# Expert layer: next block turned one weight unit ahead, first expert's rows selected by matmuls on chip

## The chip, the cores and the metric

One core of one Trainium2 chip. The time is device microseconds (us) of one execution. PE is TensorE (PEld its weight load), ACT is ScalarE, DVE is VectorE, POOL is GpSimd, SP is SyncE, which issues most DMAs.

## The reference, cut to what matters

Two decoder layers run on 256 prompt rows and 8 sample rows, 264 rows of 1024 numbers. Layer 1 ends in a layer of 8 experts: each row goes to the two experts with the highest router logits.

```python
logits = h @ w_router + b_router
top_v, top_i = lax.top_k(logits, 2)
gates = softmax(top_v)
for e in range(8):
    act = silu(h @ we_gate[e]) * (h @ we_up[e])
    out = out + combine[..., e:e + 1] * (act @ we_down[e])
```

`h` is RMSNorm(x) of the layer's rows; an expert's hidden width is 1408. All numbers are float32.

## The kernel before, in words

**Numbers in two parts.** Every large product is made of three: an operand is split into a high part (rounded to float32r, a form of float32 that PE takes in one pass) and a low part (what the rounding left), and high x high, high x low and low x high are added in PSUM. For weights, ACT writes the high part (`whi`, lines 899 and 1085) and DVE the low part (`low`, line 309) of a *unit*, up to 2048 columns on 128 partitions, 1 MB. `raw` and `low` share six buffers, `whi` has three: high part c waits until unit c-3 has been used by PE (line 1084), and the DMA of unit c (line 430) until unit c-6 has (line 423).

**The experts.** An expert is 18 units (lines 94 to 102): gate and up projections (units 0 to 7, and 10 to 13), down projections (8, 9, and 14 to 17). Expert 0 is written out, experts 1 to 7 run in a loop on each engine. Work on one expert needs its block of 128 chosen rows, transposed: `ehi` and `elo`, 8 tiles of 128x128 in high and low parts. The next expert's block is made near the end of the one before: PE transposes it out of `xe` in `gather_turn` (lines 782 to 786, before the flow of units 16 and 17), ACT writes `ehi` out of PSUM (`take_turned`, 1087 to 1091, its last step of an expert) and DVE `elo` (`turned_low`, 1655 to 1660, likewise). Only then do ACT and DVE split the next expert's units. PE's first product of an expert waits for `ehi`, `elo` and unit 0 (lines 825 to 829).

**The routing ahead of expert 0.** When the last group of layer 1 is done, PE transposes x into token rows (`route_turns`, 502 to 508; half 0 into PSUM banks 1 to 3, half 1 into 4 to 6) and makes the router's logits; DVE takes the rows' statistics (1212 to 1219), picks two experts per row, and works out in `offf` and `offi` where each row goes (lines 1594 to 1632). ACT writes the normed token rows `xn` (1114). POOL scatters them to the DRAM buffer `xs` with six indirect DMAs (1877 to 1881); SP waits for all six, then reads block 0 back into `xe` (417, 418). PE transposes it (866) and expert 0 begins.

Of the kernel before, what the change touches and what calls it, by code (L numbers as in the profile page):

```python
# [22 lines left out]
P = 128  # L23
D = 1024
KT = D // P
# [3 lines left out]
DEPTH = 2  # L29
# [88 lines left out]
LG0, BI0, RK0 = 0, 32, 64  # L118
COLS0 = 272
# [5 lines left out]
def build(nc, a, out):  # L125
    ctx = ExitStack()
    with ctx:
# [7 lines left out]
        with ExitStack() as same:  # L135
# [84 lines left out]
        xn = sb("xn", [P, 3, D], where=moe)  # L220
        picked = sb("picked", [P, 2, 3, D], where=moe)
# [25 lines left out]
        cnti = sb("cnti", [P, 1], I32, where=moe)  # L247
        moe.close()
# [32 lines left out]
            "row_out", "col_ps", "col_done", "zero_done", "filled", "xn_done", "xtok_done", "off_done", "scattered", "gates_done", "fin_gain",  # L281
# [72 lines left out]
        def _(sp):  # L354
# [96 lines left out]
        def _(pe):  # L451
# [282 lines left out]
            for l in range(DEPTH):  # L734
# [47 lines left out]
            def gather_turn(it):  # L782
                pe.wait_ge(S["xe_in"], it * 16 + 16)
# [4 lines left out]
            def expert(it):  # L788
# [36 lines left out]
                pe.wait_ge(S["ehi_done"], it + 1)  # L825
                pe.wait_ge(S["elo_done"], it + 1)
# [28 lines left out]
                turn_hidden(2, 2)  # L855
                down(15)
                gather_turn(it + 1)
# [5 lines left out]

            pe.wait_ge(S["xtok_done"], 6)
            pe.wait_ge(S["off_done"], 1)
            gather_turn(0)
# [12 lines left out]
        def _(act):  # L879
# [207 lines left out]
            def take_turned(it):  # L1087
                act.wait_ge(S["xeT_ps"], it + 1)
                for k in range(KT):
                    last = act.activation(ehi[:, k, :], ps[:, 6 + k // 4, (k % 4) * P:(k % 4 + 1) * P], ACT.Copy, scale=N_(k, NORM_ROW[3]))  # L1090
                last.then_inc(S["ehi_done"], 1)
# [19 lines left out]
            for j, (_, n) in enumerate(TILES):  # L1111
                for half in range(2):
                    c = slice(half * PB, (half + 1) * PB)
                    act.activation(xn[0:n, j, c], token_rows(j, half, n), ACT.Copy, scale=rcol[0:n, j:j + 1]).then_inc(S["xn_done"], 1)
            expert_hi(0, 2)
            act.wait_ge(S["top_done"], 1)
            act.activation(gt[:, :, 1:2], gt[:, :, 0:1], ACT.Exp).then_inc(S["gate_exp"], 1)
# [45 lines left out]
            take_turned(0)  # L1163
            expert(0)
# [19 lines left out]
        def _(dve):  # L1184
# [111 lines left out]
            def layer(l):  # L1296
# [233 lines left out]
                else:  # L1530
                    expert_lo(0, 0)
                    expert_lo(0, 1)
                dve.wait_ge(used, U + 12)
# [41 lines left out]
            dve.wait_ge(S["moe_const"], 4)  # L1575
            dve.wait_ge(S["stored"], 16 * STORES * DEPTH)
            dve.wait_ge(S["cs_out"], 64 * DEPTH)
            dve.wait_ge(S["tT_ps"], 1)
            token_statistics(0)
# [52 lines left out]
            dve.tensor_copy(offi[:, :], offf[:, :]).then_inc(S["off_done"], 1)  # L1632

# [12 lines left out]
            dve.tensor_copy(cnti[:, :], cnt[:, 2:3]).then_inc(S["rounds"], 1)  # L1646
            expert_lo(0, 2)
# [7 lines left out]
            def turned_low(it):  # L1655
                dve.wait_ge(S["ehi_done"], it + 1)
                for k in range(KT):
                    last = dve.scalar_tensor_tensor(elo[:, k, :], ps[:, 6 + k // 4, (k % 4) * P:(k % 4 + 1) * P], N_(k, NORM_ROW[3]),  # L1658
                                                    ehi[:, k, :].bitcast(F32), ALU.mult, ALU.subtract)
                last.then_inc(S["elo_done"], 1)  # L1660
# [40 lines left out]
            turned_low(0)  # L1701
# [29 lines left out]
        def _(pool):  # L1731
# [140 lines left out]
            settle()  # L1872
            pool.memset(chosen[:, :, :], 0.0).then_inc(S["moe_const"], 1)
# [41 lines left out]
```

## Time and profile before

| | |
|---|---|
| median of 3 runs | 1043.75 us (1042.79 to 1044.28) |
| the profiled execution | 1043.59 us, of which the span of instructions is 1041.8 us |
| busy | PE 890.4 us (85%), DVE 756.9 (73%), ACT 540.2 (52%), POOL 181.4 (17%) |
| chain that ended last | PE 68%, DVE 23%, DMA 3%, issue 3%, ACT 3% |
| DMA | 240.38 MB, mean 231 GB/s; 322 to 368 GB/s in the slices from 600 us to the end of the experts |

A row of the trace gives when an instruction started, how long it took, and in brackets how long its engine had been idle and what ended that. Rows of PE overlap: the distance between two starts is what a product costs in a stream. The granted clock is 1.00 at 2.4 GHz and 0.50 at 1.2 GHz.

### The profile page before, as it was taken

The page shows a single profiled execution, that of the slowest core. Times are in us where ns is not written, and L with a number is a line of the kernel's source. Part 1 is how long each engine was busy: PE and PEld are TensorE (multiplying, and loading weights), DVE is VectorE, ACT ScalarE, POOL GpSimd, SP SyncE. Part 2 cuts the span into 40 slices and gives each one's busy share as a digit, 9 for nine tenths or more (in the row PEclk, how much of TensorE's full clock was granted, in tenths as well). Part 3 has the DMA queues.
Part 4 walks back from the last instruction along what each step waited for, and adds up shares of the span by engine and source line. Part 5 has one row for each costly group of instructions (what it writes and reads, how often), then busy time and mean ns, then how long its engine had stood idle before and what let it go on. Part 6 is the DMA issues. An engine that isn't in the chain of part 4 may idle for free.

```text
span 1041.8 us, 14010 instructions
## 1 busy us (share of the span) xinstructions
PE 890.4 (85%) x5260; PEld 775.1 (74%) x5260; DVE 756.9 (73%) x945; ACT 540.2 (52%) x541; POOL 181.4 (17%) x228
## 2 busy tenths in 40 slices
PE   4967777899999999877786498989898989898970
PEld 3965746899999999867475387878787878787860
DVE  3599986465566346899866287878788888788856
ACT  5425631444344335265323277667677777677750
POOL 1299123300000002992231100000000000000001
PEclk9989878899999999998688699999999999999995
DMA  9470104996536559611044399999999999999933
GB/s 308 136 234 21 62 10 125 365 414 213 182 118 226 169 179 265 214 40 42 11 135 148 129 353 335 356 322 366 326 361 341 362 345 368 333 354 348 357 131 125
DMA packets 116749, 240.38 MB, mean 231 GB/s; under 512 B 12772, under 2 KB 35062, under 8 KB 116685
## 3 DMA queue, kind: packets, MB, share of 16 engines
q1 hardware_dynamic: 107213, 207.28, 57.8%
q0 software_dynamic: 8048, 27.16, 7.5%
q10 hardware_dynamic: 1440, 5.28, 1.3%
q8 instruction: 33, 0.54, 0.2%
q14 instruction: 15, 0.12, 0.0%
HBM read 214.23 MB, written 26.04 MB: 231 GB/s over the span
## 4 chain that ended last, share of the span: by engine, by line
PE 68%; DVE 23%; DMA 3%; issue 3%; ACT 3%; POOL 0%; POOLq 0%; ACTq 0%; DVEq 0%
PE ps L537 9%; PE ps L538 9%; PE ps L539 9%; PE ps L799 8%; PE ps L801 8%; PE ps L800 8%; DVE low L309 3%; PE ps L813 3%; PE ps L815 3%; PE ps L814 3%; DVE ac L1233 3%; DVE cb L1233 2%; DVE Cs L1474 2%; ACT ehi L1090 1%; DVE elo L1658 1%
## 5 line engine op out<-in xcount | busy, mean ns | idle before, releaser
L309 DVE TENSOR_TENSOR low<-raw,whi 128x2048 fp32r<-128x2048 f32 (+2 forms) x204 | 433.5, 2135 | 109.5 <-ACT whi L1085 63.0
L1085 ACT ACTIVATE whi<-raw 128x2048 fp32r<-128x2048 f32 (+1 forms) x144 | 254.2, 1781 | 96.2 <-PE ps L801 57.0
L537 PE MATMUL ps<-nhi,whi 128*128 128x264 f32 x736 | 216.3, 294 | 11.2 <-DVE low L309 6.3
L538 PE MATMUL ps<-nlo,whi 128*128 128x264 f32 x736 | 213.7, 290 | 0.0
L539 PE MATMUL ps<-nhi,low 128*128 128x264 f32 x736 | 212.6, 289 | 0.0
L899 ACT ACTIVATE whi<-raw 128x2048 fp32r<-128x2048 f32 (+1 forms) x60 | 109.4, 1825 | 119.0 <-PE ps L539 119.0
L799 PE MATMUL ps<-whi,ehi 128*128 128x512 f32 (+1 forms) x384 | 149.1, 388 | 22.5 <-DVE low L309 18.0
L537 PEld LDWEIGHTS ps<-nhi,whi 128*128 128x128 f32 x736 | 143.6, 195 | 14.0 <-issue 12.4
L801 PE MATMUL ps<-whi,elo 128*128 128x512 f32 (+1 forms) x384 | 146.8, 382 | 0.0
L800 PE MATMUL ps<-low,ehi 128*128 128x512 f32 (+1 forms) x384 | 146.7, 382 | 0.0
L538 PEld LDWEIGHTS ps<-nlo,whi 128*128 128x128 f32 x736 | 143.7, 195 | 0.1
L539 PEld LDWEIGHTS ps<-nhi,low 128*128 128x128 f32 x736 | 142.9, 194 | 0.0
L799 PEld LDWEIGHTS ps<-whi,ehi 128*128 128x128 f32 x384 | 73.8, 192 | 37.4 <-ACT whi L1085 20.8
L801 PEld LDWEIGHTS ps<-whi,elo 128*128 128x128 f32 x384 | 73.8, 192 | 12.0
L800 PEld LDWEIGHTS ps<-low,ehi 128*128 128x128 f32 x384 | 74.0, 193 | 11.6
L1885 POOL TENSOR_TENSOR cnt<-cnt 128x1 f32<-128x1 f32 x1 | 0.2, 193 | 435.7 <-DMA xs<-ysb 435.7
L813 PE MATMUL ps<-whi,fhi 128*128 128x512 f32 x176 | 71.6, 407 | 5.1 <-DVE flo L1679 5.1
L815 PE MATMUL ps<-whi,flo 128*128 128x512 f32 x176 | 69.5, 395 | 0.0
L814 PE MATMUL ps<-low,fhi 128*128 128x512 f32 x176 | 69.4, 394 | 0.0
L1797 POOL TENSOR_SCALAR Cp<-apad,prm 128x256 f32<-128x256 f32 x48 | 52.9, 1111 | 0.0
L538 PE MATMUL ps<-hlo,whi 128*128 128x264 f32 x176 | 50.1, 284 | 0.0
L537 PE MATMUL ps<-hhi,whi 128*128 128x264 f32 x176 | 50.0, 284 | 0.0
(367 smaller groups left out, 1226.7 us busy)
## 6 DMA issues: line engine op xcount, KB each, us to landing
raw<-in_we_down SPq DMA_DIRECT2D x40, 1024.0 KB, 6.1
raw<-in_we_gate SPq DMA_DIRECT2D x32, 1024.0 KB, 7.5
raw<-in_we_up SPq DMA_DIRECT2D x32, 1024.0 KB, 7.0
raw<-in_w_in SPq DMA_DIRECT2D x16, 1024.0 KB, 5.9
xs<-zero POOLq DMA_DIRECT2D x5, 2560.0 KB, 30.2
raw<-in_we_gate SPq DMA_DIRECT2D x16, 768.0 KB, 7.5
raw<-in_we_up SPq DMA_DIRECT2D x16, 768.0 KB, 5.7
raw<-in_w_gate SPq DMA_DIRECT2D x10, 1024.0 KB, 5.2
```

The source lines that it names most:

```text
L309: return engine.tensor_tensor(low[:, u % NRAW, part], raw[:, u % NRAW, part], whi[:, u % NHI, part].bitcast(F32), ALU.subtract)
L537: pe.matmul(o, hi[:, k, c], xhi[:, kx, :], start=first, stop=False)
L538: pe.matmul(o, hi[:, k, c], xlo[:, kx, :], start=False, stop=False)
L539: last = pe.matmul(o, lo[:, k, c], xhi[:, kx, :], start=False, stop=end)
L799: pe.matmul(bank(b, w), ehi[:, k0 + k, :], hi[:, k, :], start=(k0 + k == 0), stop=False)
L800: pe.matmul(bank(b, w), ehi[:, k0 + k, :], lo[:, k, :], start=False, stop=False)
L801: last = pe.matmul(bank(b, w), elo[:, k0 + k, :], hi[:, k, :], start=False, stop=(k0 + k == KT - 1))
L813: pe.matmul(bank(4 + half), fh, hi[:, k, s], start=(t == 0), stop=False)
L814: pe.matmul(bank(4 + half), fh, lo[:, k, s], start=False, stop=False)
L815: last = pe.matmul(bank(4 + half), fl, hi[:, k, s], start=False, stop=(t == 10))
L899: act.activation(whi[:, u % NHI, 0:n], raw[:, u % NRAW, 0:n], ACT.Copy).then_inc(hi_done, 1)
L1085: act.activation(whi[:, c % NHI, 0:kt * w], raw[:, c % NRAW, 0:kt * w], ACT.Copy).then_inc(hi_done, 1)
```

## The change

**Next block one unit ahead.** In every expert PE runs `gather_turn(it + 1)` right after `turn_hidden(2, 2)`, before unit 15 instead of after it. `take_turned` and `turned_low` now signal after each half (4 of 8 tiles), so that DVE can start on the first half while ACT does the second.

**Expert 0's rows on chip.** ACT first writes the normed token rows as a float32r high part `thi`, DVE the low part `tlo`; DVE compares `offf` with a row of places 0 to 127 and gets `sel`, a matrix of zeros and ones (128 rows of a tile by 128 places). For each of 8 column tiles and 3 row tiles PE multiplies `thi` and `tlo` with `sel` and adds them up: 48 products of 128 columns, which leave the transposed block in banks 7 and 0. `xn` follows, each piece after its `tlo`; the scatter stays, for the experts that follow. SP no longer reads block 0; its wait for the scatter moves to where it reads block 1 (ahead of unit 10 of expert 0).

**Order around it.** PE's `route_turns(0)` moves ahead of the last weight unit of layer 1, DVE's statistics of that half too; high part 2 of expert 0, its low part and the exponential of the gates move behind `take_turned(0)` and `turned_low(0)`. `thi` and `tlo` lie where `picked` is at the end of the program.

```diff
@@ stream, on SP
                     if c == NRAW and isinstance(it, int) and it == 0:
-                        sp.wait_ge(S["scattered"], 96)
-                        sp.dma_start(xe[:, :], xs[0]).then_inc(S["xe_in"], 16)
+                        sp.wait_ge(S["moe_const"], 5)
                         sp.dma_start(gain[:, :], ...)
                     if c == 10:
+                        if isinstance(it, int) and it == 0:
+                            sp.wait_ge(S["scattered"], 96)
                         sp.wait_ge(S["xeT_ps"], it + 1)
                         sp.dma_start(xe[:, :], block_of(xs, it + 1)).then_inc(S["xe_in"], 16)
@@ end of layer 1, on PE
                     group(25, nhi, nlo, (0,))
                     route_logits(0)
+                    route_turns(0)
                     group(25, nhi, nlo, (1,))
-                    route_turns(0)
@@ expert, on PE
-                pe.wait_ge(S["ehi_done"], it + 1)
-                pe.wait_ge(S["elo_done"], it + 1)
+                pe.wait_ge(S["elo_done"], it * 2 + 2)
...
                 down(14)
                 turn_hidden(2, 2)
+                gather_turn(it + 1)
                 down(15)
-                gather_turn(it + 1)
@@ ahead of expert 0, on PE
+            pe.wait_ge(S["sel_done"], 3)
+            for j, (_, n) in enumerate(TILES):
+                for half in range(2):
+                    pe.wait_ge(S["tT_lo"], 2 * j + half + 1)
+                    for k in range(4 * half, 4 * half + 4):
+                        o, d = ps[:, FIRST_TURNED[half], (k % 4) * P:(k % 4 + 1) * P], slice(k * P, (k + 1) * P)
+                        pe.matmul(o, thi[0:n, j, d], sel[0:n, j, :], start=(j == 0 and k % 4 == 0), stop=False)
+                        last = pe.matmul(o, tlo[0:n, j, d], sel[0:n, j, :], start=False, stop=(j == 2 and k % 4 == 3))
+            last.then_inc(S["xeT_ps"], 1)
             pe.wait_ge(S["xtok_done"], 6)
-            pe.wait_ge(S["off_done"], 1)
-            gather_turn(0)
@@ take_turned, on ACT (turned_low on DVE alike)
-                for k in range(KT):
-                    last = act.activation(ehi[:, k, :], ps[:, 6 + k // 4, ...], ACT.Copy, scale=N_(k, NORM_ROW[3]))
-                last.then_inc(S["ehi_done"], 1)
+                for half in range(2):
+                    b = FIRST_TURNED[half] if isinstance(it, int) and it == 0 else 6 + half
+                    for k in range(4 * half, 4 * half + 4):
+                        last = act.activation(ehi[:, k, :], ps[:, b, ...], ACT.Copy, scale=N_(k, NORM_ROW[3]))
+                    last.then_inc(S["ehi_done"], 1)
@@ after the places are known, on DVE
+            for j, (_, n) in enumerate(TILES):
+                step(dve.tensor_scalar(sel[0:n, j, :], places[0:n, :], offf[0:n, 2 * j:2 * j + 1], None, ALU.is_equal))
+            settle()
+            for j, (_, n) in enumerate(TILES):
+                dve.scalar_tensor_tensor(sel[0:n, j, :], places[0:n, :], offf[0:n, 2 * j + 1:2 * j + 2], sel[0:n, j, :].bitcast(F32),
+                                         ALU.is_equal, ALU.add).then_inc(S["sel_done"], 1)
+            for j, (_, n) in enumerate(TILES):
+                for half in range(2):
+                    c = slice(half * PB, (half + 1) * PB)
+                    dve.wait_ge(S["tT_hi"], 2 * j + half + 1)
+                    dve.scalar_tensor_tensor(tlo[0:n, j, c], token_rows(j, half, n), rcol[0:n, j:j + 1], thi[0:n, j, c].bitcast(F32),
+                                             ALU.mult, ALU.subtract).then_inc(S["tT_lo"], 1)
```

How the rows of three places stand, by engine. First PE in the loop over the experts, from the transposes of the last hidden tiles (`hm`) to unit 16; before:

```order
L821 MATMUL ps<-ident,hm 128x128 [waits hm_done]
L821 MATMUL ps<-ident,hm 128x128 x2
...
L813 MATMUL ps<-whi,fhi 128x512 [waits lo_done,hi_done]
L814 MATMUL ps<-low,fhi 128x512
L815 MATMUL ps<-whi,flo 128x512
...
L785 MATMUL ps<-ident,xe 128x128 [waits xe_in]
L785 MATMUL ps<-ident,xe 128x128 x7
```

and in the change:

```order
L828 MATMUL ps<-ident,hm 128x128 [waits hm_done]
L828 MATMUL ps<-ident,hm 128x128 x2
...
L792 MATMUL ps<-ident,xe 128x128 [waits xe_in]
L792 MATMUL ps<-ident,xe 128x128 x7
...
L820 MATMUL ps<-whi,fhi 128x512 [waits lo_done,hi_done]
L821 MATMUL ps<-low,fhi 128x512
L822 MATMUL ps<-whi,flo 128x512
```

The eight transposes of the next block (`xe`) have moved in front of the twelve products of unit 15.

DVE between the places of the rows (`offi`) and expert 0; before:

```order
L1632 CAST offi<-offf 128x6 [waits dve_step]
L1638 COPY xtok<-ps 128x512 [waits xn_done] x4
L1638 COPY xtok<-ps 8x512 [waits xn_done] x2
...
L309 TENSOR_TENSOR low<-raw,whi 128x2048 [waits hi_done]
...
L1658 SCALAR_TENSOR_TENSOR elo<-ps,prm,ehi 128x128 [waits ehi_done]
L1658 SCALAR_TENSOR_TENSOR elo<-ps,prm,ehi 128x128 x7
```

and in the change:

```order
L1662 CAST offi<-offf 128x6 [waits dve_step]
L1664 TENSOR_SCALAR sel<-places,offf 128x128 x2
L1664 TENSOR_SCALAR sel<-places,offf 8x128
L1667 SCALAR_TENSOR_TENSOR sel<-places,offf,sel 128x128 [waits dve_step]
L1667 SCALAR_TENSOR_TENSOR sel<-places,offf,sel 128x128
L1667 SCALAR_TENSOR_TENSOR sel<-places,offf,sel 8x128
L1673 SCALAR_TENSOR_TENSOR tlo<-ps,rcol,thi 128x512 [waits tT_hi] x4
L1673 SCALAR_TENSOR_TENSOR tlo<-ps,rcol,thi 8x512 [waits tT_hi] x2
L1680 COPY xtok<-ps 128x512 [waits xn_done] x4
L1680 COPY xtok<-ps 8x512 [waits xn_done] x2
...
L1606 SCALAR_TENSOR_TENSOR elo<-ps,prm,ehi 128x128 [waits ehi_done]
```

Twelve instructions, `sel` and `tlo`, stand new ahead of the copies `xtok`, and `elo` comes ahead of low part 2.

ACT from the square root of the statistics to expert 0; before:

```order
L1109 ACTIVATE rcol<-ms 128x3 [waits ms_done]
L1114 ACTIVATE xn<-ps,rcol 128x512 [waits col_done]
L1114 ACTIVATE xn<-ps,rcol 128x512 x3
L1114 ACTIVATE xn<-ps,rcol 8x512 x2
L1085 ACTIVATE whi<-raw 128x2048 [waits unit_used,raw_in2]
L1117 ACT_TABLE_LOAD
L1117 ACTIVATE gt<-gt 128x3 [waits top_done]
L1090 ACTIVATE ehi<-ps,prm 128x128 [waits xeT_ps]
```

and in the change:

```order
L1124 ACTIVATE rcol<-ms 128x3 [waits ms_done]
L1129 ACTIVATE thi<-ps,rcol 128x512 [waits col_done]
L1129 ACTIVATE thi<-ps,rcol 128x512 x3
L1129 ACTIVATE thi<-ps,rcol 8x512 x2
L1134 ACTIVATE xn<-ps,rcol 128x512 [waits tT_lo] x4
L1134 ACTIVATE xn<-ps,rcol 8x512 [waits tT_lo] x2
L1105 ACTIVATE ehi<-ps,prm 128x128 [waits xeT_ps]
L1098 ACTIVATE whi<-raw 128x2048 [waits unit_used,raw_in2]
```

The six `thi` stand where `xn` stood, `xn` waits for the low parts, and high part 2 comes behind `ehi`.

## Rows read from the trace of the kernel before

**Rows 1.** Windows; columns: window, length, busy (count) PE PEld DVE ACT POOL, clock, DMA, GB/s
```profile
567.00:583.00 16.00, 0.05 (x3) 0.00 (x0) 8.01 (x23) 4.40 (x6) 7.58 (x6) 0.50 0.49 186
...
589.50:593.50 4.00, 4.00 (x10) 3.13 (x11) 0.00 (x0) 0.00 (x0) 0.00 (x0) 0.50 0.00 0
```

**Rows 2.** Chain of waits from 558 to 625 us; columns: start, length, what
```profile
577.26 2.49 DMA xs<-xn,offi
...
579.76 3.15 DMA xe<-xs
...
583.05 1.95 PE ps L785 x8
...
589.50 0.77 PE ps L799
```

**Rows 3.** Timeline of DVE and ACT during the routing; columns: start, length, instruction [idle <-releaser]
```profile
558.25 1.25 DVE L1534 TENSOR_TENSOR xT<-xT,ps 128x1056 f32<-128x1056 f32 x1 [3.64 <-PE ps L539]
...
559.66 3.67 DVE L1215 BATCH_NORM_STATS2 bst<-ps 128x6 f32<-128x512 f32 x6 [0.15 <-PE ps L507]
...
568.54 0.17 DVE L1632 CAST offi<-offf 128x6 uint32<-128x6 f32 x1
...
568.62 3.66 DVE L1638 COPY xtok<-ps 128x512 f32<-128x512 f32 x6
...
564.58 3.53 ACT L1114 ACTIVATE xn<-ps,rcol 128x512 f32<-128x512 f32 x6 [0.24 <-DVE rcol L1592]
```

**Rows 4.** Timeline of PE: two 264-column products in a row; two 128-column products
```profile
546.85 0.28 PE L537 MATMUL ps<-nhi,whi 128*128 128x264 f32 x1
...
546.97 0.28 PE L538 MATMUL ps<-nlo,whi 128*128 128x264 f32 x1
...
480.67 0.38 PE L624 MATMUL ps<-qT,kT 128*128 128x128 f32 x2
...
480.89 0.60 PE L623 MATMUL ps<-qT,kT 128*128 128x256 f32 x2
```

**Rows 5.** Waits of PE from 560 us on; columns: total us, times, longest
```profile
PE ps L799 <- DVE low L309: 18.0, 7, 2.6
```

**Rows 6.** Timeline of PE, ACT and DVE where expert 0 ends and expert 1 begins
```profile
635.23 1.04 PE L785 MATMUL ps<-ident,xe 128*128 128x128 f32 x8
...
643.01 0.47 PE L799 MATMUL ps<-whi,ehi 128*128 128x512 f32 x1 [2.57 <-DVE low L309]
...
633.03 1.05 ACT L1085 ACTIVATE whi<-raw 128x1024 fp32r<-128x1024 f32 x1
...
636.30 2.18 ACT L1090 ACTIVATE ehi<-ps,prm 128x128 fp32r<-128x128 f32 x8 [2.22 <-PE ps L785]
...
638.32 5.56 ACT L1085 ACTIVATE whi<-raw 128x2048 fp32r<-128x2048 f32 x3
...
634.39 1.22 DVE L309 TENSOR_TENSOR low<-raw,whi 128x1024 fp32r<-128x1024 f32 x1
...
638.51 2.16 DVE L1658 SCALAR_TENSOR_TENSOR elo<-ps,prm,ehi 128x128 fp32r<-128x128 f32 x8 [2.90 <-ACT ehi L1090]
...
640.59 6.69 DVE L309 TENSOR_TENSOR low<-raw,whi 128x2048 fp32r<-128x2048 f32 x3
```

**Rows 7.** Windows: three whole experts, and 3.4 us after a stop
```profile
749.20:802.50 53.30, 50.22 (x229) 41.74 (x229) 42.82 (x33) 37.08 (x34) 0.00 (x0) 0.97 0.95 341
...
802.50:854.50 52.00, 48.81 (x230) 40.69 (x230) 42.88 (x33) 37.26 (x34) 0.00 (x0) 1.00 1.00 354
...
854.50:906.30 51.80, 48.68 (x229) 40.66 (x230) 42.86 (x33) 37.13 (x34) 0.00 (x0) 1.00 1.00 353
...
695.90:699.30 3.40, 3.40 (x9) 2.66 (x10) 3.40 (x2) 0.80 (x1) 0.00 (x0) 0.51 0.96 343
```

**Rows 8.** Window: four microseconds with weights queued
```profile
656.00:660.00 4.00, 4.00 (x20) 3.18 (x19) 3.41 (x4) 2.32 (x2) 0.00 (x0) 1.00 1.00 401
```

**Rows 9.** Waits of ACT from 590 to 1005 us
```profile
ACT whi L1085 <- DMA raw<-in_we_down: 6.8, 6, 1.8
```

More of the change, by code:

```diff
@@ L118 @@
 LG0, BI0, RK0 = 0, 32, 64
+FIRST_TURNED = (7, 0)
 COLS0 = 272
@@ L220, in build @@
         xn = sb("xn", [P, 3, D], where=moe)
+        with ExitStack() as early:
+            thi = sb("thi", [P, 3, D], F32R, where=early)
+            tlo = sb("tlo", [P, 3, D], F32R, where=early)
         picked = sb("picked", [P, 2, 3, D], where=moe)
@@ L247, in build @@
         cnti = sb("cnti", [P, 1], I32, where=moe)
+        places = sb("places", [P, P], where=moe)
+        sel = sb("sel", [P, 3, P], F32R, where=moe)
         moe.close()
@@ L1088, in take_turned @@
                 act.wait_ge(S["xeT_ps"], it + 1)
-                for k in range(KT):
-                    last = act.activation(ehi[:, k, :], ps[:, 6 + k // 4, (k % 4) * P:(k % 4 + 1) * P], ACT.Copy, scale=N_(k, NORM_ROW[3]))
-                last.then_inc(S["ehi_done"], 1)
+                for half in range(2):
+                    b = FIRST_TURNED[half] if isinstance(it, int) and it == 0 else 6 + half
+                    for k in range(4 * half, 4 * half + 4):
+                        last = act.activation(ehi[:, k, :], ps[:, b, (k % 4) * P:(k % 4 + 1) * P], ACT.Copy, scale=N_(k, NORM_ROW[3]))
+                    last.then_inc(S["ehi_done"], 1)
             def y_rows(it):
@@ L1113, in _ @@
                     c = slice(half * PB, (half + 1) * PB)
+                    act.activation(thi[0:n, j, c], token_rows(j, half, n), ACT.Copy, scale=rcol[0:n, j:j + 1]).then_inc(S["tT_hi"], 1)
+            for j, (_, n) in enumerate(TILES):
+                for half in range(2):
+                    c = slice(half * PB, (half + 1) * PB)
+                    act.wait_ge(S["tT_lo"], 2 * j + half + 1)
                     act.activation(xn[0:n, j, c], token_rows(j, half, n), ACT.Copy, scale=rcol[0:n, j:j + 1]).then_inc(S["xn_done"], 1)
-            expert_hi(0, 2)
-            act.wait_ge(S["top_done"], 1)
-            act.activation(gt[:, :, 1:2], gt[:, :, 0:1], ACT.Exp).then_inc(S["gate_exp"], 1)
             def expert(it):
@@ L1163, in _ @@
             take_turned(0)
+            expert_hi(0, 2)
+            act.wait_ge(S["top_done"], 1)
+            act.activation(gt[:, :, 1:2], gt[:, :, 0:1], ACT.Exp).then_inc(S["gate_exp"], 1)
             expert(0)
@@ L1532, in layer @@
                     expert_lo(0, 1)
+                    dve.wait_ge(S["moe_const"], 5)
+                    dve.wait_ge(S["stored"], 16 * STORES * DEPTH)
+                    dve.wait_ge(S["cs_out"], 64 * DEPTH)
+                    dve.wait_ge(S["tT_ps"], 1)
+                    token_statistics(0)
                 dve.wait_ge(used, U + 12)
@@ L1574, in _, with turned_low @@
             layer(1)
[L1575 to L1579, printed above, removed]
+            def turned_low(it):
+                for half in range(2):
+                    b = FIRST_TURNED[half] if isinstance(it, int) and it == 0 else 6 + half
+                    dve.wait_ge(S["ehi_done"], it * 2 + half + 1)
+                    for k in range(4 * half, 4 * half + 4):
+                        last = dve.scalar_tensor_tensor(elo[:, k, :], ps[:, b, (k % 4) * P:(k % 4 + 1) * P], N_(k, NORM_ROW[3]),
+                                                        ehi[:, k, :].bitcast(F32), ALU.mult, ALU.subtract)
+                    last.then_inc(S["elo_done"], 1)
             dve.wait_ge(S["tT_ps"], 2)
@@ L1634, in _ @@
             for j, (_, n) in enumerate(TILES):
+                step(dve.tensor_scalar(sel[0:n, j, :], places[0:n, :], offf[0:n, 2 * j:2 * j + 1], None, ALU.is_equal))
[4 more added lines that the diff above has]
+            for j, (_, n) in enumerate(TILES):
+                for half in range(2):
+                    c = slice(half * PB, (half + 1) * PB)
+                    dve.wait_ge(S["tT_hi"], 2 * j + half + 1)
+                    dve.scalar_tensor_tensor(tlo[0:n, j, c], token_rows(j, half, n), rcol[0:n, j:j + 1], thi[0:n, j, c].bitcast(F32),
+                                             ALU.mult, ALU.subtract).then_inc(S["tT_lo"], 1)
+            for j, (_, n) in enumerate(TILES):
                 for half in range(2):
@@ L1653, in _ @@
             dve.tensor_tensor(gt[:, :, 3:4], gt[:, :, 1:2], gt[:, :, 2:3], ALU.mult).then_inc(S["gates_done"], 1)
[L1655 to L1660, printed above, removed]
             def expert(it):
@@ L1872, in _ @@
             settle()
+            pool.iota(places[:, :], pattern=[[1, P]], base=0, channel_multiplier=0, allow_small_or_imprecise_dtypes=True).then_inc(S["moe_const"], 1)
             pool.memset(chosen[:, :, :], 0.0).then_inc(S["moe_const"], 1)
```

6 lines of the change are left out of this document (3 added, 3 removed).

## The prediction

> **What bounds the kernel now.** I read the windows first, to see where PE stands still; then the chain of waits and the timelines at those places; then windows of single experts, to see what else is near its limit. Nothing before 545 us is touched by the change, nor the last 33 us, so the answer lies in two places.
>
> The first is the way from routing to expert 0. From 567 to 583 us PE is busy 0.05 us [rows 1]. The chain shows why: the last scatter lands (from 577.26 us, 2.49 us), block 0 is read back (3.15 us), PE turns it (8 transposes in 1.95 us), ACT and DVE write `ehi` and `elo`, and the first product starts at 589.50 [rows 2]. For its first 4 us the clock is granted at 0.50, which is 1.2 GHz [rows 1].
>
> The second is the border between experts. PE waits there seven times, 18.0 us in total [rows 5]; the border after expert 0 stands for all. The transposes start at 635.23, `ehi` takes ACT 2.18 us, `elo` takes DVE 2.16 us after that, and only at 640.59 does DVE come to low part 0; PE resumes at 643.01 after 2.57 us [rows 6]. Work that three engines do one after another stands in front of a unit that they could split meanwhile. Some of these stops cost twice: after the one at 693 us the clock is 0.51 for 3.4 us, in which PE starts 9 products [rows 7]. That costs half of 3.4 us, 1.7 us. Of the six experts between borders, three (one stands in the rows, 53.30 us at a mean clock of 0.97) hold such a dip, and undisturbed ones last 51.8 to 52.0 us [rows 7].
>
> **The border, step by step,** on the clock of the old trace. With the transposes ahead of unit 15 they are over at about 633.4, while ACT still makes high part 17 (633.03 for 1.05 us, to 634.1 [rows 6]). ACT then writes `ehi` at once instead of idling 2.22 us: halves at 635.2 and 636.3. DVE is free at 635.6 (low part 17, 634.39 for 1.22 us [rows 6]) and follows half by half, done at 637.8. What is late next is unit 15, pushed back by 0.9 us of transposes: its `whi` buffer is the one that high part 0 needs, so ACT starts that at 636.3 and ends at 638.2 (1.85 us each, three in 5.56 us [rows 6]); low part 0 takes 2.2 us (three in 6.69 us [rows 6]), to 640.5. PE, finished at 640.45, goes on at about 640.7. The stop shrinks from 2.57 to about 0.3 us: 2.3 us at each of seven borders, 16.1 us. Even stops of 2.57 us are followed by a dip only at three of the borders [rows 7], so at 0.3 us I take none: three dips less, 5.1 us. Together 21.2 us.
>
> That is not free of the DMA. An undisturbed expert moves 354 GB/s for 52.0 us, 18.4 MB, with the DMA engines busy all the time [rows 7]. PE alone would need 52.0 - 2.6 = 49.4 us. If 354 GB/s is the ceiling, no border gives anything in an undisturbed expert. If it is the 401 GB/s of four microseconds with weights queued [rows 8], 18.4 MB take 45.9 us and nothing is lost. I take the middle, 377 GB/s or 48.8 us: PE stays the slower one on the mean, but only just, and weights arrive unevenly. ACT already waits for down weights, six times and up to 1.8 us [rows 9], and the shorter border takes 2.3 us of slack from those units. For this I give back 0.8 us per expert, 5.6 us in seven, nearer to none than to all, because today's waits hardly reach PE. The experts then save 15.4 us; the ends are 21.2 and, at a ceiling of 354 GB/s, the dips' 5.1.
>
> The Trainium skill speaks against this part: "DMA: Bandwidth & Descriptors", section "Where 436 GB/s comes from", puts the HBM side at about 358 GB/s per core. By that figure 18.4 MB take an estimated 51.4 us per expert and the borders would give almost nothing. The trace's 401 GB/s over 4 us does not agree with such a limit, its 353 and 354 over whole experts do.
>
> **Routing.** *The moved turns.* Twelve transposes of `route_turns(0)` (0.11 us each: eight at full clock are busy for 1.04 us with the last one's tail [rows 6]) go ahead of the last weight unit, 1.3 us. Before, they ran beside the addition at 558.25 (1.25 us [rows 3]). In exchange three of six statistics (3.67 us for six [rows 3]) leave the path. From the addition's start to the last statistic took 5.08 us; now 1.25 for the addition, 1.5 for the other twelve transposes and 1.85 for three statistics, 4.7. Net the routing gets 1.0 us *later*: `offi` is ready at 569.7, not 568.7.
>
> *The selection on DVE.* Six `sel` operations of 128 columns, priced at most like `elo` (2.16 us for 8 [rows 6]), 1.6 us; six `tlo` out of PSUM like the `xtok` copies (3.66 us for 6 [rows 3]), 3.7 us. They start at 569.7 and end at 575.0. ACT's `thi` replaces `xn` one for one (3.53 us [rows 3]) and hides there. Then come the copies `xtok` (3.7 us) and the counts (0.5), so DVE cannot begin `elo` before 579.2.
>
> *The selection on PE.* No row shows a float32r product of 128 columns. Bounds at 2.4 GHz: 0.06 us, the 264-column product of 0.12 us [rows 4] scaled to 128 columns; and 0.22 us, a plain float32 product of that shape, which the trace shows as two passes of 0.11 us [rows 4]. I take one pass, 0.11 us: it is one record of the same shape, and 128 columns may not amortise a weight load that 264 do. At 1.2 GHz I take 0.244 us (the transposes of rows 2). PE starts at 571.9 after 4 us of rest, so at 1.2 GHz; as before expert 0 [rows 1] I give it 4.0 us there, 16 products, and the other 32 take 3.5 us: the block is there at 579.4. `ehi` 2.2 us, the second half of `elo` 1.1 us behind it, and PE starts expert 0 at 582.9 instead of 589.5. **Saved: 6.6 us.** With 0.06 us DVE's copies decide, and it starts at 581.5 (8.0 saved); with 0.22 us the block is there at 584.5 and it starts at 587.9 (1.6 saved).
>
> The Trainium skill ("TensorE: Matmul & The Clock Gate", section "Back-to-back issue gap") gives about 81 ns per product of 128 columns with its weight load. By that, 48 products take an estimated 3.9 us and the start lies near the early bound. No run here shows that form.
>
> *What costs nothing.* The scatter now starts when `xn` does, some 4 us later, and ends near 584; SP wants it for block 1, ahead of unit 10, which is four units of PE work, some 13 us, after 582.9. High and low part 2 fall behind `elo` and are done by 586, while PE works on units 0 and 1 until 590. The earlier load of `gain` uses DMA engines that are half idle [rows 1]. If these covers went, each would cost PE its own lateness, a few us once.
>
> **Sum.** 1043.6 us (the profiled execution; 0.2 us under the median, which I leave aside) - 15.4 - 6.6 = **1021.6 us**. With every cost at its low end 1043.6 - 21.2 - 8.0 = 1014.4; at its high end 1043.6 - 5.1 - 1.6 = 1036.9.
>
> **Rivals.** *Weights at the ceiling.* The DMA cannot exceed 354 GB/s and takes the place of the border. For it: DMA share 1.00 in both undisturbed experts [rows 7]. Against: 401 GB/s [rows 8], and no PE stop but the border in them that the weights cause. 1043.6 - 5.1 - 6.6 = 1031.9. The rule of the Trainium skill quoted above would lead to this case.
>
> *Dear selection.* The 128-column products cost 0.22 us. For it: every plain product of that shape does [rows 4]. Against: the 264-column float32r rows run twice as fast per column. 1043.6 - 15.4 - 1.6 = 1026.6.
>
> *Border unchanged.* Something other than the row turns holds unit 0, so the stop stays; 1043.6 - 6.6 = 1037.0. Against it: every step of that border is accounted for above.
>
> *Slower.* With no rest at the border the queue of weights never empties and the rate itself falls. The experts last 419.7 us now (589.5 to 1009.2). They undo the 6.6 us if they average 53.3 us, that is below 345 GB/s; at the 341 GB/s of the dipped expert [rows 7] they take 54.0 us each, 12 us more, and the total is 1049. Against it: that expert was slow because PE asked for less, and the fuller ones run at 353 and 354.
>
> **Numbers.** Forecast 0.60, ceiling 0.19, dear selection 0.14, border unchanged 0.04, slower 0.03. The range reaches from the low end, 1014, past the ceiling case to 1032, and leaves out the last two cases and part of the mixed one, in which ceiling and dear selection meet. A difference under 0.2% is about what a measurement of this kernel cannot tell from none. Faster 0.96, same 0.01, slower 0.03.
>
> **What would show it.** Right: seven border waits under 0.5 us each, none under a dipped clock; first expert product near 583; ACT waiting longer for weights than the rows of today, PE stops of about a microsecond at the first down unit. Wrong: experts of 51.5 us or more at a DMA share of 1.00 (ceiling); the 48 products spread over 12 us (dear selection); the border waits still over 2 us; or a PE start after 589.5.

## The result, and the profile after

The changed kernel takes **1020.42 us** (median of 4 runs, 1018.20 to 1021.47) against 1044.01 us of the kernel before (4 runs, 1042.79 to 1044.59): a ratio of 0.9773, with a 95% interval of 0.9752 to 0.9793. The forecast was 1021.6 us. The total fits, but it comes from two terms that were wrong by about as much in opposite directions.

| us | before | after | difference |
|---|---|---|---|
| span of the profiled execution | 1041.8 | 1016.4 | -25.4 |
| up to expert 0's first product | 589.50 | 586.43 | -3.1 |
| experts, first to last product | 419.7 | 397.6 | -22.1 |
| behind the last product | 32.65 | 32.41 | -0.2 |

The border first. The waits of PE between 585 and 990 us in the trace of the changed kernel (total us, times, longest), which answer to [rows 5]:

```profile
PE ps L820 <- DVE flo L1716: 4.4, 8, 0.6
PE ps L806 <- issue: 3.5, 1, 3.5
PE ps L806 <- DVE low L315: 1.6, 7, 0.2
```

18.0 us in seven waits have become 1.6 us; the longest is 0.2. The timeline where expert 0 ends and expert 1 begins (start, length, instruction, idle before it) answers to [rows 6]:

```profile
629.38 1.04 PE L792 MATMUL ps<-ident,xe 128*128 128x128 f32 x8
...
629.97 1.05 ACT L1098 ACTIVATE whi<-raw 128x1024 fp32r<-128x1024 f32 x1
630.87 0.55 DVE L1716 TENSOR_TENSOR flo<-ps,fhi 128x384 fp32r<-128x384 f32 x1
630.92 2.16 ACT L1105 ACTIVATE ehi<-ps,prm 128x128 fp32r<-128x128 f32 x8
631.34 1.22 DVE L315 TENSOR_TENSOR low<-raw,whi 128x1024 fp32r<-128x1024 f32 x1
632.47 2.15 DVE L1606 SCALAR_TENSOR_TENSOR elo<-ps,prm,ehi 128x128 fp32r<-128x128 f32 x8
635.21 2.29 DVE L315 TENSOR_TENSOR low<-raw,whi 128x2048 fp32r<-128x2048 f32 x1 [0.59 <-ACT whi L1098]
...
637.65 0.47 PE L806 MATMUL ps<-whi,ehi 128*128 128x512 f32 x1 [0.22 <-DVE low L315]
```

ACT goes from high part 17 (L1098 at 629.97) into `ehi` without a pause, where it had stood 2.22 us. Low part 0 still ends last, but PE stands 0.22 us for it instead of 2.57.

Windows (length, busy time of PE, PEld, DVE, ACT and POOL, clock, DMA share, GB/s) from the routing to expert 3 answer to [rows 1] and [rows 7]; the last two are whole experts (1 and 3):

```profile
567.00:583.00 16.00, 10.90 (x52) 10.56 (x52) 11.70 (x39) 6.39 (x12) 5.71 (x6) 0.59 0.34 136
586.40:590.40 4.00, 3.97 (x9) 3.14 (x10) 2.72 (x4) 2.06 (x3) 0.00 (x0) 0.50 0.02 4
...
637.65:687.17 49.52, 48.72 (x230) 40.66 (x230) 43.00 (x32) 37.39 (x34) 0.00 (x0) 1.00 1.01 373
736.65:786.18 49.53, 48.73 (x230) 40.68 (x230) 43.00 (x32) 37.28 (x34) 0.00 (x0) 1.00 0.99 365
```

An expert takes 49.5 us at a clock of 1.00 and moves its weights at 365 to 373 GB/s. None of the seven periods from one expert's first product to the next one's (49.46 to 49.67 us, and 51.2 for expert 0, which starts at the low clock) holds a further clock dip. The transfers had not been at a ceiling.

Now the routing, in the chain of waits from 556 to 600 us, which answers to [rows 2] and [rows 3]:

```profile
559.89 1.26 DVE xT L1559
561.20 1.54 PE ps L514 x12
562.76 1.89 DVE bst L1235 x3
...
570.02 0.58 DVE sel L1664 x3
570.63 0.86 DVE sel L1667 x3
571.49 0.67 DVE tlo L1673
572.30 0.45 PE ps L876
573.17 0.21 PE ps L877
...
582.96 3.47 issue
586.43 0.77 PE ps L806
```

Scatter and read-back are gone from the chain. In their place stand the 48 selection products, 572.30 to 582.96 us, and behind them 3.47 us that the view calls issue and that are `ehi` and `elo`. The products are 0.21 us apart but for one step of 0.35, where those with 8 rows begin. The window that holds them alone, between that of the 5 us before 570 and that of the 396 us from 590.4 on, says at which clock:

```profile
565.00:570.00 5.00, 0.55 (x7) 0.38 (x7) 4.05 (x33) 3.81 (x8) 0.00 (x0) 0.99 0.11 44
...
572.30:583.00 10.70, 10.66 (x48) 10.35 (x48) 7.11 (x14) 3.86 (x7) 5.71 (x6) 0.50 0.51 202
...
590.40:986.00 395.60, 387.63 (x1824) 323.56 (x1822) 336.95 (x253) 294.75 (x263) 0.00 (x0) 1.00 0.97 354
```

The granted clock was 0.50, that is 1.2 GHz, for all 48. It fell at 569.9 us (the 0.99 of the first window), when PE had been busy for 0.55 of the 5 us before, and came back at 590.4, four microseconds into expert 0.

### The profile page after: what moved, and what is told of

The parts are those of the page before. It is cut to its first block, busy times and chain, and to the rows that moved or that the text cites. A ratio compares the mean times of both kernels' runs of the same rounds, so it can differ in the third digit from the quotient of the medians.

```text
span 1016.4 us, 14109 instructions
## 1 busy us (share of the span) xinstructions
PE 895.7 (88%) x5300; PEld 780.7 (77%) x5300; DVE 764.1 (75%) x957; ACT 544.9 (54%) x547; POOL 179.8 (18%) x229
## 4 chain that ended last, share of the span: by engine, by line
PE 72%; DVE 22%; ACT 3%; issue 2%; DMA 1%; POOL 0%; POOLq 0%; DVEq 0%; ACTq 0%
PE ps L544 10%; PE ps L545 9%; PE ps L546 9%; PE ps L806 8%; PE ps L808 8%; PE ps L807 8%; DVE low L315 3%; PE ps L820 3%; PE ps L822 3%; PE ps L821 3%; DVE ac L1253 3%; DVE cb L1253 2%; PE ps L664 1%; ACT whi L1098 1%; DVE Cs L1494 1%
## 5 line engine op out<-in xcount | busy, mean ns | idle before, releaser
L1098 ACT ACTIVATE whi<-raw 128x2048 fp32r<-128x2048 f32 (+1 forms) x144 | 254.9, 1775 | 85.4 <-PE ps L808 38.0
L806 PE MATMUL ps<-whi,ehi 128*128 128x512 f32 (+1 forms) x384 | 147.0, 383 | 5.1 <-issue 3.5
```

The lines of the kernel that those rows point to most:

```text
L806: pe.matmul(bank(b, w), ehi[:, k0 + k, :], hi[:, k, :], start=(k0 + k == 0), stop=False)
L1098: act.activation(whi[:, c % NHI, 0:kt * w], raw[:, c % NRAW, 0:kt * w], ACT.Copy).then_inc(hi_done, 1)
```

## The experiments

All twelve ran beside runs of the kernel before on the same chip; ratios are to those. Where a start moves by a microsecond or two, medians of runs that spread over 2 to 3 us are a poor ruler. I also use the time within the profiled execution from the first addition to `xT` behind the last mixer (DVE; 544.48 us before, 544.84 after) to expert 0's first product: 45.02 us before, 41.59 after, and 41.58 to 41.67 in the four other kernels with the change's routing unaltered. The expectations call it the xT-to-first-product time.

### One half of the change at a time

`border_only` is the kernel before with these edits (ACT and DVE hand over `ehi` and `elo` in halves as in the change):

```diff
-                down(15)
                 gather_turn(it + 1)
+                down(15)
```

> Edit: the kernel before, with only the border half of the change (next block turned one unit ahead of down(15), ehi and elo signalled in halves); the routing and the reading back from DRAM stay. Theory (what the trace of the changed kernel shows is additive: 22.1 us of its 25.4 us lie between the first and the last expert product): about 1044.0 - 22 = 1022 us, expert periods 49.5 us, borders 0.2 us, and the first expert product still near 589.5 us. The prediction's own term (21.2 us less 5.6 us given back to the weight transfers): 1028.6 us with periods near 50.5 us. Rival (the earlier start of the experts or the removed DRAM traffic is what lets the weights keep up): periods above 50.5 us here although the border is the same.

1023.47 us (1022.33 to 1024.31), ratio 0.9789 (0.9760 to 0.9818). The experts take 398.7 us and their windows are those of the changed kernel:

```profile
690.00:740.00 50.00, 49.20 (x233) 41.16 (x232) 43.53 (x33) 37.48 (x34) 0.00 (x0) 1.00 1.01 369
```

So this half is worth 21 us by itself, on the old read-back; 1.1 us of that are the halves at expert 0, as the traces of the next run show. The give-back of 5.6 us to the transfers is not there, nor does the border need the other half.

`routing_only` is the changed kernel with the border undone (DVE's wait for `ehi` alike):

```diff
-                gather_turn(it + 1)
                 down(15)
+                gather_turn(it + 1)
...
-                    last.then_inc(S["ehi_done"], 1)
+                    if isinstance(it, int) and it == 0:
+                        last.then_inc(S["ehi_done"], 1)
+                    elif half == 1:
+                        last.then_inc(S["ehi_done"], 2)
```

> Edit: the changed kernel with the border put back (turn behind down(15), ehi and elo handed over whole; the first block keeps its halves). Theory: the routing half alone is worth what the first expert product moved, 589.50 to 586.43: 3.1 us, so about 1041 us, with the border wait of 2.6 us back at seven borders. The prediction's term was 6.6 us: 1037.4 us. Rival: the routing half alone is worth nothing, 1044 us, since the weights that it starts sooner are waited for later.

1040.38 us (1039.27 to 1042.52), ratio 0.9962 (0.9946 to 0.9978): 4 us, and 3.4 us by the xT-to-first-product time (41.58 us). The seven stops at the border are back:

```profile
PE ps L806 <- DVE low L315: 17.9, 7, 2.6
```

Not all of the 3.4 us is the selection. With the old routing that time was 45.02 us in the kernel before and 43.87 in `border_only`, and the timelines show where the two part, first the kernel before, then `border_only`:

```profile
585.03 2.18 ACT L1090 ACTIVATE ehi<-ps,prm 128x128 fp32r<-128x128 f32 x8 [13.60 <-PE ps L785]
...
587.24 2.16 DVE L1658 SCALAR_TENSOR_TENSOR elo<-ps,prm,ehi 128x128 fp32r<-128x128 f32 x8 [11.83 <-ACT ehi L1090]
```

```profile
587.38 2.17 ACT L1090 ACTIVATE ehi<-ps,prm 128x128 fp32r<-128x128 f32 x8 [13.53 <-PE ps L785]
...
588.55 2.16 DVE L1659 SCALAR_TENSOR_TENSOR elo<-ps,prm,ehi 128x128 fp32r<-128x128 f32 x8 [10.72 <-ACT ehi L1090]
```

From the places (`offi`) to PE's transposes both take the same, 14.51 and 14.44 us, so the read-back is constant. From the start of `ehi` to the first product it is 4.47 us before and 3.39 in `border_only`, where `elo` follows half by half. There, ahead of expert 0, PE waits for `elo` itself, and the halves are worth 1.1 us; the selection with its moved turns is worth the other 2.3 us (43.87 to 41.59). Both runs hold the halves at expert 0, so their gains, 20.9 and 4.0 us, count this 1.1 us twice, which is most of what they add up to above the 23.6 of the whole change.

### Which part of the border

`no_halves` keeps the early turn and hands `ehi` and `elo` over whole (the second piece of the diff above); `turn_late` keeps the halves and turns behind `down(15)` (the first piece).

> Edit: the changed kernel, where ehi and elo of the next block are again handed over whole and not in halves; the turn stays ahead of down(15). Theory (the unit of down products of about 2.6 us that now lies behind the turn hides the 2.57 us by itself): the border grows from 0.2 us to at most 1.2 us, 1020.4 to 1027 us, most likely near 1021. Rival (both parts are needed): each border about 1.1 us, which is half of ACT's eight copies of 2.2 us, 1028 us, or more where clock dips return.

1020.20 us (1019.19 to 1021.04), ratio 0.9759 (0.9730 to 0.9789), as fast as the changed kernel, with the same waits at the border:

```profile
PE ps L806 <- DVE low L315: 1.6, 7, 0.2
```

> Edit: the changed kernel with the turn put back behind down(15); ehi and elo stay in halves. Theory: the halves hide about 1.1 us of the old border wait of 2.57 us, so each of seven borders keeps 1.2 to 1.5 us: 1020.4 + 7 x 1.35 = 1030 us, and 1035 us if the three clock dips return. Rival (the halves alone would have done): within 2 us of the changed kernel, 1022 us.

1038.11 us (1035.17 to 1039.60), ratio 0.9932 (0.9910 to 0.9955). The theory expected 1030 to 1035, since the halves would hide 1.1 us of each border. They hide 0.26: PE's waits there are 16.1 us over seven borders, where `routing_only` has 17.9.

```profile
PE ps L806 <- DVE low L315: 16.1, 7, 2.3
```

The timeline of the border at 740 us says why:

```profile
738.01 2.17 ACT L1105 ACTIVATE ehi<-ps,prm 128x128 fp32r<-128x128 f32 x8 [2.21 <-PE ps L792]
...
739.18 2.16 DVE L1606 SCALAR_TENSOR_TENSOR elo<-ps,prm,ehi 128x128 fp32r<-128x128 f32 x8 [2.11 <-ACT ehi L1105]
...
740.02 5.56 ACT L1098 ACTIVATE whi<-raw 128x2048 fp32r<-128x2048 f32 x3
...
742.02 4.49 DVE L315 TENSOR_TENSOR low<-raw,whi 128x2048 fp32r<-128x2048 f32 x2 [0.68 <-ACT whi L1098]
...
744.46 0.47 PE L806 MATMUL ps<-whi,ehi 128*128 128x512 f32 x1 [2.30 <-DVE low L315]
```

`elo` is done at 741.3, but DVE then waits 0.68 us for high part 0, which ACT makes after all of `ehi`. What PE waits for is the next unit's split behind the turn, not the turn. Halves shorten a handover that does not end last; the early turn moves ACT's whole queue forward. All of the border's gain is the one moved line; halves pay only where PE waits for `elo` itself, ahead of expert 0. The total came out above the theory because 2.3 us remain at each border and two of the three clock dips are back in the trace (0.50 and 0.52 for 3.4 us from 951.9 and from 692.6 us). `turn_late` also shows that a DMA share near 1 proves no ceiling: the expert from 744.46 to 796.05 us has a share of 0.99 at 355 GB/s, those after the change 1.01 at 373.

### How near the transfers are

`no_low_weights` leaves out the products with the weights' low parts in all experts, a third of PE's work there (the low parts are still made):

```diff
-                        pe.matmul(bank(b, w), ehi[:, k0 + k, :], lo[:, k, :], start=False, stop=False)
...
-                            pe.matmul(bank(4 + half), fh, lo[:, k, s], start=False, stop=False)
```

> Edit: the changed kernel without the products of the low part of the weights in all experts (a third of PE's work there is left out; the low parts are still made). Theory (the weight transfers still have room at the changed kernel's period of 49.5 us, 371 GB/s): the period falls, to the 43 us that DVE is busy per expert or to 46 us, which is 18.4 MB at the 401 GB/s seen in one window of the kernel before; 8 x 4 = 28 us off, near 990 us. Rival (with the border gone the transfers are the bound, as the DMA share of 1.0 in the changed kernel's windows suggests): the period stays at 49 to 49.5 us, 1016 to 1020 us. Third (the ceiling of 354 GB/s that the prediction allowed): 52 us, which the changed kernel has already gone below.

1000.15 us (a single run). With PE out of the way an expert takes 47.4 to 47.9 us and not the 43 or 46 hoped for; one of them:

```profile
777.36:825.03 47.67, 38.79 (x160) 29.41 (x160) 42.65 (x33) 36.95 (x34) 0.00 (x0) 0.93 1.03 387
```

No engine is busy all the time, the DMA is, at 387 GB/s, and ACT now waits for weights, 25.9 us in four experts against 8.0 us in five of the changed kernel; half of it are the down weights:

```profile
ACT whi L1096 <- DMA raw<-in_we_down: 13.3, 13, 2.0
```

The changed kernel's 49.5 us are thus PE's, with some 2 us per expert between them and this rate. The room is there, but little of it is left. Whether the transfers could do more than 387 GB/s over an expert no run here shows.

### What the selection costs

`turns_back` puts the first twelve turns and their statistics back:

```diff
-                    route_turns(0)
                     group(25, nhi, nlo, (1,))
+                    route_turns(0)
```

> Edit: the changed kernel with the first twelve turns to token rows and their statistics put back behind the last unit, as before. Theory (the move costs the routing 0.95 us: from the first xT addition to the places 25.01 us after, 24.06 before): the first expert product comes 0.95 us sooner, 1019.5 us. Rival (the twelve turns that no longer stand ahead of PE's last unit keep PE busy later, and the statistics, three of 0.62 us, come behind it): 0 to 1 us later, 1020.4 to 1021.4 us.

1020.75 us (1020.70 to 1021.00), ratio 0.9769 (0.9743 to 0.9796). In the trace `offi` comes 24.06 instead of 25.01 us after the addition and the first product 40.65 instead of 41.59, as expected; the total doesn't show it. One part of it went back to the clock, which rose 4.8 instead of 4.0 us after the first product: expert 0's first six units, up to its first turn of hidden columns, took 19.46 instead of 19.05 us. The rest is inside the spread between runs.

`halfwise` orders low parts, products, rows and copies by halves of the columns, with a signal behind the first half:

```diff
-            for j, (_, n) in enumerate(TILES):
-                for half in range(2):
-                    pe.wait_ge(S["tT_lo"], 2 * j + half + 1)
+            for half in range(2):
+                for j, (_, n) in enumerate(TILES):
+                    pe.wait_ge(S["tT_lo"], 3 * half + j + 1)
...
-            last.then_inc(S["xeT_ps"], 1)
+                last.then_inc(S["half_ps"] if half == 0 else S["xeT_ps"], 1)
```

> Edit: the changed kernel with the low parts, the selection products, the normalised rows and the row copies in the order half by half (all three token tiles of columns 0 to 511, then of 512 to 1023) and a signal behind the first half, so that ACT and DVE take ehi and elo of it while PE selects the other. Theory: of the 3.47 us between the last selection product and the first expert product 1.1 to 1.6 us go (half of ACT's and DVE's eight copies of 2.17 us each): xT-to-first-product 40.2 instead of 41.6 us, 1019.1 us. Rival (ACT or DVE is busy with rows and copies then, so nothing moves): 1020.4 us.

1019.23 us (1018.13 to 1021.24), ratio 0.9750 (0.9723 to 0.9777); 40.95 instead of 41.59 us to the first product. The gap behind the products shrinks from 3.47 to 2.44 us, but the products end 0.4 us later behind the places, since PE now changes between 128-row and 8-row products three times instead of once, and each time the next two starts are 0.34 and 0.27 us apart instead of 0.21.

`awake` adds products that nobody reads, so that PE does not rest:

```diff
+            def keep_awake(n, b):
+                for _ in range(n):
+                    pe.matmul(bank(b, PB), nhi[:, 0, 0:P], whi[:, 0, 0:PB], start=True, stop=True)
...
             last.then_inc(S["col_ps"], 1)
+            pe.wait_ge(hi_done, ND + 1)
+            keep_awake(10, 0)
...
+            keep_awake(16, 0)
             pe.wait_ge(S["sel_done"], 3)
...
             pe.wait_ge(S["xtok_done"], 6)
+            keep_awake(14, 1)
             expert(0)
```

> Edit: the changed kernel with products added that nobody reads (128x512, stationary and moving from tiles at hand, into a bank that is rewritten later): 10 while PE waits for the choice of experts, 16 while it waits for the selection, 14 between the selection and the first expert product. Theory (a 128x128 selection product takes 0.213 us only because the granted clock is 0.5 from the routing on, 0.107 us at 1.0): the 48 products take 5.1 instead of 10.7 us, the block is ready 5.4 us sooner, and the first expert products run at 0.23 instead of 0.43 us (1.8 us more): 1020.4 - 7.2 = 1013.2 us, xT-to-first-product time 36.2 instead of 41.6 us. Rival (a product of this form costs 0.21 us at any clock): only the 1.8 us, 1018.6 us. Second rival (the added products don't keep the clock up, and run at 0.43 us each in front of the selection): 1020 to 1026 us.

1016.87 us (1015.82 to 1019.95), ratio 0.9737 (0.9705 to 0.9769), and 39.68 us to the first product: half of what the theory promised for the total (3.6 of 7.2 us), and 1.9 of 5.4 us up to the first product. The timeline of PE shows both why it is right and why it falls short:

```profile
573.22 0.27 PE L882 MATMUL ps<-sel,thi 128*128 128x128 f32 x1
573.33 0.27 PE L883 MATMUL ps<-sel,tlo 128*128 128x128 f32 x1
...
577.69 0.41 PE L882 MATMUL ps<-sel,thi 8*128 8x128 f32 x1
577.90 0.41 PE L883 MATMUL ps<-sel,tlo 8*128 8x128 f32 x1
...
579.76 5.59 PE L772 MATMUL ps<-whi,nhi 128*128 128x512 f32 x14 [0.17 <-DVE xtok L1687]
```

At a clock of 1.0 a selection product takes 0.11 us, so "0.21 us at any clock" falls. But at 577.5 us, 4.5 us into the products, with PE idle for 0.4 us since 566, the clock falls all the same, and the last 9 products cost 0.21 again. The 14 added ones then run at the low clock up to 584.3 and hold PE until 585.19, 2.2 us longer than `elo` (ready at 582.96) needed.

`halfwise_awake` has both edits, with 8 added products at the end:

> Edit: both of the other two together, with 8 instead of 14 added products behind the selection. Theory (the two add up): 1013.2 - 1.4 = 1011.8 us, xT-to-first-product 34.8 us; with faster products the low parts of DVE (4.02 us for six) come to bound the selection, so at most 1 us of this may be missing. Rival (clock not held): as halfwise, 1019.1 us, or up to 1025 us.

1014.69 us (1013.46 to 1015.22), ratio 0.9706 (0.9679 to 0.9734); 38.12 us to the first product. That is 3 us short of the theory and better than the rival, since the clock holds for a part. It falls in the same place, in the middle of the products, and returns 0.7 us into expert 0:

```profile
572.10:576.60 4.50, 4.50 (x38) 4.36 (x39) 4.50 (x8) 4.50 (x9) 1.05 (x1) 1.00 0.02 4
576.60:579.10 2.50, 2.50 (x12) 2.33 (x11) 2.45 (x6) 0.36 (x2) 1.89 (x3) 0.50 0.71 283
579.20:582.70 3.50, 3.50 (x9) 2.77 (x9) 2.70 (x10) 3.41 (x6) 2.62 (x3) 0.50 0.93 379
```

### The selection the other way round

`rowwise` takes `sel` as the stationary operand and lets 512 columns of `thi` or `tlo` move: 12 products instead of 48. The selected rows come out unturned; ACT copies them to `xe` and PE turns them.

```diff
-                        pe.matmul(o, thi[0:n, j, d], sel[0:n, j, :], ...)
-                        last = pe.matmul(o, tlo[0:n, j, d], sel[0:n, j, :], ...)
+                    pe.matmul(bank(FIRST_TURNED[half], PB), sel[0:n, j, :], thi[0:n, j, c], ...)
+                    last = pe.matmul(bank(FIRST_TURNED[half], PB), sel[0:n, j, :], tlo[0:n, j, c], ...)
...
+                    last = pe.transpose(ps[:, FIRST_TURNED[half], ...], xe[:, k * P:(k + 1) * P], ident[:, :])
...
+                act.activation(xe[:, half * PB:(half + 1) * PB], bank(FIRST_TURNED[half], PB), ACT.Copy)...
```

> Edit: the kernel of the run halfwise_awake, where the selection is multiplied the other way round (sel stationary, 512 columns of thi or tlo moving: 12 products instead of 48), the selected rows are copied to xe by ACT and turned by eight transposes; the second half of the normalised rows and of the row copies comes behind ehi and elo, and PE waits for the last row copies only ahead of its first turn of hidden columns. Theory (in the trace of halfwise_awake 48 products of 128 columns take 5.3 us at a granted clock of 1.0 and 0.21 us each once it falls; 512 columns take 0.23 us at 1.0): the selection ends with the last low part, and the first expert product comes 10.5 us behind the places instead of 12.7: 1014.7 - 2.2 = 1012.5 us. Rival (the extra copy and turns, one behind the other through PE, ACT, PE, ACT and DVE, eat what the products give): 1014 to 1017 us.

1012.54 us (1011.21 to 1013.35), ratio 0.9689 (0.9673 to 0.9706); 35.41 us to the first product, which comes 10.40 us behind the places. By the ratios it can hardly be told from `halfwise_awake`, by the traces its first product comes 2.7 us sooner. The clock never falls, in these windows and up to the end of the experts:

```profile
570.00:582.00 12.00, 10.87 (x49) 6.88 (x46) 10.85 (x34) 7.75 (x19) 0.00 (x0) 1.00 0.00 1
582.00:586.00 4.00, 4.00 (x17) 3.29 (x18) 3.83 (x7) 3.97 (x5) 3.14 (x3) 1.00 0.51 204
586.00:979.00 393.00, 386.38 (x1816) 321.87 (x1815) 337.75 (x257) 292.74 (x261) 7.42 (x4) 1.00 0.98 360
```

`rowwise_plain` is the same without the added products.

> Edit: the kernel of the run rowwise without the 34 products that nobody reads. Theory (the added products are what keep the clock at 1.0 between the routing and the experts, the other way of multiplying saves by itself): the granted clock falls near 570 us again and stays low into the first expert; each pair of 512-column products then takes 0.86 us where a low part comes every 0.67 us, so the selection ends 1.1 us later, the eight turns take 0.5 us longer and the first expert products lose 2 us: 1012.5 + 3.6 = 1016 us, xT-to-first-product time 37 instead of 35.4 us. Rival (512 columns are work enough, the clock never falls or comes back during the selection): 1012.5 to 1013.5 us.

1016.46 us (1015.50 to 1019.03), ratio 0.9737 (0.9718 to 0.9756); 38.33 us to the first product. The total is as the theory had it, the two parts are not: 2.9 us are lost up to the first product and 0.8 in the experts, where it had 1.6 and 2.

```profile
573.00:579.00 6.00, 6.00 (x12) 3.05 (x12) 4.70 (x8) 2.24 (x4) 0.00 (x0) 0.50 0.00 0
583.60:587.60 4.00, 3.97 (x10) 3.14 (x11) 3.83 (x7) 3.71 (x4) 3.16 (x3) 0.50 0.51 211
```

The turned-round products, with the halves and the later rows, save 3.3 us of 41.59 at the low clock; the clock held up by the added products saves another 2.9, and 0.8 us in the experts (397.93 to 397.13). The low clock is a cost of its own, and without the work in the gaps it stays.

`rowwise_turns` is `rowwise` with the first twelve turns behind the last unit, as in `turns_back`.

> Edit: the kernel of the run rowwise with the first twelve turns to token rows and their statistics put back behind the last unit. Theory (the move costs 0.95 us of the routing, as the trace of turns_back shows up to the first expert product, and its total could not show it beside a low clock that lasted 3.4 us longer): xT-to-first-product 34.4 instead of 35.4 us, 1011.6 us. Rival (as in turns_back, the gain is taken back by the clock or within the run-to-run spread): 1012.5 us or more, with a clock dip between 560 and 590 us.

1011.57 us (1010.65 to 1013.15), ratio 0.9691 (0.9675 to 0.9708). The first product comes after 34.46 us, 0.95 us sooner, and the clock holds. It is the fastest trace (span 1009.0 us); its median is 1 us below `rowwise`, but the two ratios can't be told apart. Both beat the changed kernel by 8 to 9 us.

## Why the prediction was right, and where it was not

**The border** was read rightly: low part 0 behind the row turn, seven stops from 2.57 to about 0.3 us (measured 0.2), three dips gone, 21.2 us (measured 22.1 for all experts, of which the stops are 18.0 - 1.6 = 16.4 us; the dips, priced at 1.7 us each, make PE busy 50.2 us instead of 48.7 to 48.8 in an expert [rows 7], an estimated 1.5 us each or 4.5 in three; the rest is in smaller waits). The step-by-step walk named ACT's high part 0 as the last link, and `turn_late` confirms it. The walk counted the halves in as well; at the border they are worth nothing beside the early turn (`no_halves`).

**The give-back to the DMA**, "0.8 us per expert, 5.6 us in seven", was the mis-sized term: it measures about zero. I put the transfers in the middle between 354 and 401 GB/s, at 377; with PE out of the way they reach 387 over whole experts. Above all, the 354 was no property of the DMA: it was 18.4 MB divided by PE's period, and rose to 365 to 373 when the period fell. ACT waits hardly longer for weights (down weights nine times, 6.9 us, beside 6.8 in six [rows 9]), and nothing of it reaches PE: the 4.4 us that PE waits at the first down unit stood in the kernel before too (5.1 us in nine waits). With the term falls the ceiling rival. The Trainium skill ("DMA: Bandwidth & Descriptors", section "Where 436 GB/s comes from") puts the HBM side at about 358 GB/s per core, which it takes as a half of the 716 GB/s of a stack that two cores share. The traces of this one core do not agree with 358 as a limit: 365 to 373 over whole experts of the changed kernel, 384 to 387 in `no_low_weights`.

**The moved turns** were priced at 1.0 us and cost 0.95. **DVE's part** was right too: the low parts were to end at 575.0 and end at 575.4.

**The selection on PE** is the step that failed: "as before expert 0 [rows 1] I give it 4.0 us there, 16 products, and the other 32 take 3.5 us". All 48 ran at 1.2 GHz, 10.7 us instead of 7.5, and the block was there at 583.0, not 579.4. The price at 2.4 GHz was right (0.11 us, `awake`), that at 1.2 GHz was 0.213 and not 0.244. The assumption that the clock returns after 4 us of any product had one row behind it, and that row was of 512-column products. The handover behind it was right, 3.3 us priced and 3.47 measured, and holds the 1.1 us of the halves. Saved were 3.1 us instead of 6.6 (3.4 from the addition to `xT` on, which the changed kernel reaches 0.4 us later); the dear-selection rival came near, by another mechanism than its own. The Trainium skill ("TensorE: Matmul & The Clock Gate", section "Back-to-back issue gap") gives about 81 ns per product of 128 columns with its weight load, and names no number format there. These float32r products do not agree: 0.111 us apart at 2.4 GHz.

So 1043.6 - 15.4 - 6.6 should have read 1043.6 - 22.1 - 3.1, less 0.2 behind the experts, which is 1018.2 us: the profiled execution. The experts gave 6.7 us more than forecast, the routing 3.5 less, and 0.2 came from the end: 3.4 us between forecast and that execution.

## What to carry to other kernels

A transfer rate taken from a stage that another engine bounds is that engine's period in other units, and a DMA share near 1 does not make it a ceiling; leaving out part of the other engine's work shows how far the rate can still rise. When a handover is moved, look at what the engines do after it: here the next unit's split behind the row turn was waited for, so moving the turn gave everything and splitting it in halves nothing; ahead of expert 0, where those splits were done long before, the halves gave 1.1 us. Work put on TensorE right behind a rest has to be priced at the clock granted there, for all of its length unless a row of the same work shows the clock coming back.

## What was not expected of the hardware

- 10.7 us of back-to-back float32r products of 128 columns at a granted clock of 0.50 did not bring the clock back, while 4 us of 512-column products did in the same trace (590.4 us).
- The clock fell in the midst of back-to-back products of that form: at 577.5 us in `awake` and at 576.6 in `halfwise_awake`, with PE busy 4.5 of the last 4.5 us. In `rowwise`, with 512-column products in their place, it did not fall. Why it fell is not shown.
- A float32r product of 128 columns takes 0.111 us at 2.4 GHz and 0.213 at 1.2, hardly less than one of 264 columns (0.12 us [rows 4]). It takes the same with 8 rows of contraction as with 128.
